# Hybrid GLA/Hyena encoder, float32: level factors in PSUM, one multiplication per level, blocks of 32 tokens, ScalarE scaling the head outputs

## The reference

```
h = rmsnorm(x);  q, k, v, r, g_lr, hyena = split(h @ w_in)
S_t = diag(exp(g_t)) S_{t-1} + k_t^T v_t ;  o_t = q_t S_t          # per head, g_t <= 0
o   = o_forward + o_backward                                        # over 256 tokens
o   = rmsnorm(o, per head) * silu(r)
x   = x + w_out([o ; hyena_group(...)])
x   = x + w_down(silu(h2 @ w_gate) * (h2 @ w_up)),  h2 = rmsnorm(x)
```

## Time and profile before

| | us |
|---|---|
| median of 3 runs | 1418.57 |
| the profiled execution, own time | 1420.57 |
| its span, first to last instruction | 1418.7 |
| PE busy | 1371.7 |
| DVE, ACT, POOL busy | 460.3, 479.1, 691.6 |
| layer 0, slots 4 to 24 | from 60 to 300 |
| layer 1, slots 4 to 24 | from 778 to 997 |

### The profile page before, as it was taken

One profiled execution on the slowest core, in us unless ns is written; L12 is line 12 of the kernel. 1 busy time (PEld: TensorE's weight loads), 2 busy tenths in 40 slices (PEclk: granted clock), 3 DMA queues, 4 the chain that ended last, 5 costly groups with the idle time before them and its releaser, 6 DMA issues.

```text
span 1418.7 us, 18349 instructions
## 1 busy us (share of the span) xinstructions
PE 1371.7 (97%) x7760; PEld 1096.4 (77%) x7760; DVE 460.3 (32%) x689; ACT 479.1 (34%) x740; POOL 691.6 (49%) x423
## 2 busy tenths in 40 slices
PE   6899999999999999999999899999999999999997
PEld 5566776788888778888876777777788888888885
DVE  5844855534022210000054776554250000000003
ACT  4644432233323223221246443322342223222122
POOL 2642753353555555544424665534625555554442
PEclk9999999999999999999999999999999999999999
DMA  6210111122323222332311211111222322233231
GB/s 234 87 44 32 60 33 59 44 67 82 127 90 104 89 90 81 113 104 90 103 60 47 73 46 61 61 45 33 86 75 89 104 96 97 90 117 105 90 104 75
DMA packets 31186, 116.63 MB, mean 82 GB/s; under 512 B 3456, under 2 KB 3584, under 8 KB 30720
## 3 DMA queue, kind: packets, MB, share of 16 engines
q1 hardware_dynamic: 31104, 115.45, 24.4%
HBM read 113.34 MB, written 2.10 MB: 81 GB/s over the span
## 4 chain that ended last, share of the span: by engine, by line
PE 85%; DVE 9%; ACT 2%; issue 1%; POOL 1%; DMA 1%; POOLq 0%; DVEq 0%; SPq 0%; ACTq 0%
PE ps L1098 16%; PE ps L1099 16%; PE ps L1100 16%; PE ps L1106 7%; PE ps L1109 7%; PE ps L1107 7%; PE ps L1314 4%; PE ps L1300 3%; PE ps L1128 2%; PE ps L1174 2%; DVE ring L925 1%; DVE ring L924 1%; PE ps L1235 1%; PE ps L1161 1%; PE ps L1261 1%
## 5 line engine op out<-in xcount | busy, mean ns | idle before, releaser
L692 POOL TENSOR_TENSOR w_lo<-w_raw,w_hi 128x1024 fp32r<-128x1024 f32 x192 | 464.1, 2418 | 412.8 <-ACT w_hi L417 412.8
L1098 PE MATMUL ps<-h_hi,w_hi 128*128 128x512 f32 (+1 forms) x1064 | 433.0, 407 | 0.4 <-POOL w_lo L692 0.4
L1100 PE MATMUL ps<-h_hi,w_lo 128*128 128x512 f32 (+1 forms) x1064 | 413.6, 389 | 0.0
L1099 PE MATMUL ps<-h_lo,w_hi 128*128 128x512 f32 (+1 forms) x1064 | 413.3, 388 | 0.0
L417 ACT ACTIVATE w_hi<-w_raw 128x1024 fp32r<-128x1024 f32 x192 | 201.7, 1051 | 197.8 <-PE ps L1109 193.6
L1098 PEld LDWEIGHTS ps<-h_hi,w_hi 128*128 128x128 f32 x1064 | 200.9, 189 | 48.8 <-issue 8.7
L1099 PEld LDWEIGHTS ps<-h_lo,w_hi 128*128 128x128 f32 x1064 | 200.7, 189 | 45.8 <-issue 7.2
L1100 PEld LDWEIGHTS ps<-h_hi,w_lo 128*128 128x128 f32 x1064 | 200.4, 188 | 42.1
L1072 DVE TENSOR_TENSOR hid<-ps,sg 128x512 f32<-128x512 f32 x44 | 30.4, 692 | 428.8 <-PE ps L1100 428.8
L1106 PE MATMUL ps<-w_hi,hid_hi 128*128 128x512 f32 x352 | 137.3, 390 | 1.9 <-POOL w_lo L692 1.9
L1107 PE MATMUL ps<-w_lo,hid_hi 128*128 128x512 f32 x352 | 137.0, 389 | 0.0
(11 more groups left out here) (154 smaller groups left out, 1559.4 us busy)
## 6 DMA issues: line engine op xcount, KB each, us to landing
w_raw<-in_units SPq DMA_DIRECT2D x198, 512.0 KB, 3.6
par<-in_par SPq DMA_DIRECT2D x2, 1310.5 KB, 9.7
gain<-in_gain SPq DMA_DIRECT2D x5, 512.0 KB, 4.8
x<-in_x SPq DMA_DIRECT2D x4, 512.0 KB, 7.2
out_y<-x SPq DMA_DIRECT2D x4, 512.0 KB, 2.6
cst<-in_cst SPq DMA_DIRECT2D x1, 1536.0 KB, 15.0
mask_f<-in_mask SPq DMA_DIRECT2D x1, 320.0 KB, 12.0
cst<-in_cst SPq DMA_DIRECT2D x1, 224.0 KB, 4.0
```

Source lines behind the costliest of these rows:

```text
L692: nc.gpsimd.tensor_tensor(w_tile(g, 1), w_raw[:, g % RAW], w_tile(g, 0).bitcast(F32), ALU.subtract).then_inc(s_lo, 1)
L1098: nc.tensor.matmul(out, hi, act_hi, start=start, stop=False)
L1099: nc.tensor.matmul(out, hi, act_lo, start=False, stop=False)
L1100: return nc.tensor.matmul(out, lo, act_hi, start=False, stop=stop)
```

## The change

1. The exponential of a level goes from `ring` to a PSUM bank instead of back to `ring`: banks 4 and 5 (`FB`), by the parity of the level number. ACT waits until DVE has used the factor two levels back.
2. DVE multiplies a whole level in one instruction: `pairs` is an access pattern that takes the lower halves from `g1` and the upper ones from `g2`; the result goes to `ring`.
3. All level results and the attention output share banks 2 and 3. Their columns are split: step 0, and the narrow results, in columns 0 to 255 or 0 to 383, level 1 and the attention output in 256 to 511.
4. The small blocks are of 32 tokens (`NEAR`) instead of 64. `near`, the masks and the put instructions are half as wide; PE runs the diagonal and the levels 3 to 7 in blocks of 32, twice as many matmuls of half the size.
5. The levels are dealt anew to the steps: (0), (1, 2), (3, 4, 5), (6, 7) instead of (0), (1, 2, 3), (4, 5), (6, 7). Level 3 loses its place in step 1, and step 2 has three levels. ACT does the third factor of a step behind the rounding of the slot's weight unit.
6. DVE runs `put_levels` ahead of `scaled`. PE runs `attend` ahead of the next head's step 0.
7. ACT scales the head outputs in 16 instructions in slot 22; DVE keeps the reciprocal (L1041).
8. `g12` starts at a multiple of 256 bytes from the base.

The core of the diff:

```diff
-STEPS = ((0,), (1, 2, 3), (4, 5), (6, 7))
+NEAR = 2 * MASKED[0]
+STEPS = ((0,), (1, 2), (3, 4, 5), (6, 7))
+PUTS = (0, 0, 0, 6)
-LA, LC = 2, 4
+LA, FB = 2, 4
+        place[0] += (base - place[0]) % 256
+        def pairs(h, s):
+            first = g1[:, h]
+            return bass.AP(first.tensor, first.offset,
+                           [list(first.ap[0]), [2 * s, TOK // (2 * s)], [HEADS * TOK + s, 2], [1, s]])
...
-            def factors(L, slot):
+            def factors(L, slot, late):
-                    for l in STEPS[hp[1]]:
+                    for l in STEPS[hp[1]][2:] if late else STEPS[hp[1]][:2]:
                         act.wait_ge(expo.sem, expo.at(L, n + 1))
-                        nc.scalar.activation(ring[:, n % FACT], ring[:, n % FACT], ACT.Exp,
+                        if n < 2:
+                            act.wait_ge(zmin.sem, zmin.at(L, HEADS))
+                        else:
+                            act.wait_ge(xld.sem, xld.at(L, n - 1))
+                        nc.scalar.activation(ps[:, FB + n % 2, :], ring[:, n % FACT], ACT.Exp,
                                              scale=1.0 / TEMP).then_inc(fact.sem, 1)
...
-                    factors(L, slot)
+                    factors(L, slot, False)
                     hi_unit(L * UNITS + slot + 2)
+                    factors(L, slot, True)
...
                     if slot == 22:
+                        act.wait_ge(o_inv.sem, o_inv.at(L, 1))
+                        for h in range(HEADS):
+                            for n in range(TT):
+                                k = TT * h + n
+                                last = nc.scalar.activation(v_tok[:, h, n], v_tok[:, h, n], ACT.Copy, scale=oss[:, k:k + 1])
+                            last.then_inc(osc.sem, 1)
                         hyena_square(L, 0)
...  # DVE, scaled
-                    f = split(ring[:, n % FACT], s)
-                    nc.vector.tensor_tensor(f[:, :, 0], split(g1[:, h], s)[:, :, 0], f[:, :, 0], ALU.mult)
-                    nc.vector.tensor_tensor(f[:, :, 1], split(g2[:, h], s)[:, :, 1], f[:, :, 1], ALU.mult)\
-                        .then_inc(xld.sem, 1)
+                    nc.vector.tensor_tensor(split(ring[:, n % FACT], s), pairs(h, s), split(ps[:, FB + n % 2, :], s),
+                                            ALU.mult).then_inc(xld.sem, 1)
...
+                    put_levels(L, slot)
                     scaled(L, slot)
-                    put_levels(L, slot)
...  # PE, level_step
-                        for e in range(2):
-                            cols = slice(P * n + BLOCK * e, P * n + BLOCK * e + BLOCK)
-                            nc.tensor.matmul(ps[BLOCK * e:BLOCK * e + BLOCK, LA, BLOCK * n:BLOCK * n + BLOCK],
-                                             g1[:, h, cols], g2[:, h, cols], start=True, stop=True)
+                        for e in range(0, P, NEAR):
+                            cols = slice(P * n + e, P * n + e + NEAR)
+                            nc.tensor.matmul(ps[e:e + NEAR, LA, NEAR * n:NEAR * n + NEAR], g1[:, h, cols], g2[:, h, cols],
+                                             start=True, stop=True)
...
-                        pe.wait_ge(put.sem, put.at(L, 10 * h + 2))
+                        pe.wait_ge(put.sem, put.at(L, 10 * h + PUTS[p]))
```

More of the change, by code:

```diff
@@ L547, in big_levels @@
                 act.wait_ge(pair.sem, pair.at(L, 4 * h + 2))
-                a = acs.next()
                 tiles = amat[:, 0].rearrange("p s j i -> p (s j) i")
-                forward, backward = (ps[:, LA + way, :].rearrange("p (l n c) -> p l n c", l=2, n=TT) for way in range(2))
-                nc.scalar.activation(near, forward[:, 0], ACT.Copy).then_inc(acs.sem, 1)
-                nc.scalar.activation(tiles[0:BLOCK, :, BLOCK:P], forward[0:BLOCK, 1], ACT.Copy)
-                nc.scalar.activation(tiles[BLOCK:P, :, 0:BLOCK], backward[BLOCK:P, 1], ACT.Copy)
-                act.wait_ge(acs.sem, a)
-                for rows in (slice(32, 64), slice(96, P)):
-                    last = nc.scalar.activation(near[rows, :, 0:32], backward[rows, 0, :, 0:32], ACT.Copy)
+                ways = [ps[:, LA + way, :] for way in range(2)]
+                nc.scalar.activation(near, ways[0][:, 0:TT * NEAR].rearrange("p (n c) -> p n c", n=TT), ACT.Copy)
+                for way in range(2):
+                    j, i = BLOCK * way, BLOCK * (1 - way)
+                    wide = ways[way][:, SEQ:2 * SEQ].rearrange("p (n c) -> p n c", n=TT)
+                    nc.scalar.activation(tiles[j:j + BLOCK, :, i:i + BLOCK], wide[j:j + BLOCK], ACT.Copy)
+                    for m in (0, BLOCK):
+                        j, i = m + NEAR * way, m + NEAR * (1 - way)
+                        narrow = ways[way][:, TT * NEAR:SEQ].rearrange("p (n c) -> p n c", n=TT)
+                        last = nc.scalar.activation(tiles[j:j + NEAR, :, i:i + NEAR], narrow[j:j + NEAR], ACT.Copy)
                 last.then_inc(big.sem, 1)
@@ L933, in put_levels @@
                 v.wait_ge(pair.sem, pair.at(L, 4 * h + p + 1))
-                if p == 1:
+                if p == 2:
                     v.wait_ge(big.sem, big.at(L, h + 1))
-                done = 10 * h + (0, 0, 2, 6)[p]
-                for l in (3,) if p == 1 else STEPS[p]:
+                done = 10 * h + PUTS[p]
+                for l in STEPS[p]:
                     for way in range(2):
@@ L1039, in _ @@
                         v.wait_ge(o_rms.sem, o_rms.at(L, 1))
[L1040 to L1047 removed]
+                        nc.vector.reciprocal(oss[:, :], oss[:, :]).then_inc(o_inv.sem, 1)
                     if slot == 24:
@@ L1198, in level_step @@
                             j, i = (low, up) if way == 0 else (up, low)
-                            last = nc.tensor.matmul(ps[:, LC + way, P * q:P * q + P], xl[rows, j], xl[rows, i],
+                            last = nc.tensor.matmul(ps[:, LA + way, P * q:P * q + P], xl[rows, j], xl[rows, i],
                                                     start=True, stop=True)
@@ L1226, in level_step @@
                     else:
-                        pe.wait_ge(put.sem, put.at(L, 10 * h + 2))
-                for l in (3,) if p == 1 else STEPS[p]:
-                    xl = ring[:, lvl(h, l) % FACT]
-                    for n in range(TT):
-                        for e in range(2):
-                            cols = slice(P * n + BLOCK * e, P * n + BLOCK * e + BLOCK)
-                            at = level_cols(l).start + BLOCK * n
-                            for way, rows in enumerate(ways):
-                                last = nc.tensor.matmul(
-                                    ps[BLOCK * e:BLOCK * e + BLOCK, level_bank(l) + way, at:at + BLOCK],
-                                    xl[rows, cols], xl[rows, cols], start=True, stop=True)
+                        pe.wait_ge(put.sem, put.at(L, 10 * h + PUTS[p]))
+                    for l in STEPS[p]:
+                        xl = ring[:, lvl(h, l) % FACT]
+                        for n in range(TT):
+                            for e in range(0, P, NEAR):
+                                cols = slice(P * n + e, P * n + e + NEAR)
+                                at = level_cols(l).start + NEAR * n
+                                for way, rows in enumerate(ways):
+                                    last = nc.tensor.matmul(ps[e:e + NEAR, LA + way, at:at + NEAR], xl[rows, cols],
+                                                            xl[rows, cols], start=True, stop=True)
                 last.then_inc(pair.sem, 1)
@@ L1329, in side @@
                 if at == 1:
+                    for h in range(HEADS):
+                        if slot == 4 * h + 8:
+                            attend(L, h)
                     hp = step_at(slot - 4)
@@ L1332, in side @@
                         level_step(L, *hp)
-                    for h in range(HEADS):
-                        if slot == 4 * h + 8:
-                            attend(L, h)
                     if slot == 22:
```

65 lines of the change are left out of this document (30 added, 35 removed).

## The result

The changed kernel takes 1408.07 us in the median of 4 runs (1407.15 to 1408.62), the kernel before 1420.00 beside it (4 runs, 1418.51 to 1422.59): a ratio of 0.9909, with a 95% interval of 0.9897 to 0.9920. It is faster by 12 to 13 us. The profiled execution has a span of 1405.4 us and 1407.15 of its own time, 13.4 less than the one before; the forecast for it was 1403.6.

A forecast was written before the change was run, and what follows sets the result against it. PE, busy 97% of the span, bounds the kernel, so only its waits and own work count. Waits 13.3, clock 4.5, PE's work -0.8: 17.0 us off 1420.57 gives 1403.6, median 1401.6; own range 1399 to 1408, 8-of-10 range 1396 to 1411.

The forecast's parts named there:

- DVE's multiplication: DVE's 128 multiplications become 64 of 512 columns with a source in PSUM, 0.65 us each; old pair 1.79 us.
- Puts: DVE's put instructions at half the columns: between 0.24 and 0.47 us each, 0.34 taken.
- L1286, 5.6: PE's wait for DVE's products in slot 19, both layers: 2.8 us each goes, gain 5.6 us.
- L1251, L1199, L1269, `oss`, 3.1: PE's smaller waits for DVE, 1.3, 0.8, 0.6 and 0.4 us: all gone, 3.1; at worst none.
- L1210, 3.2 with 0.3 left: PE's 3.5 us wait in slot 5, layer 1: scans end about 1.2 us sooner; gain 3.2, between 2.0 and 3.5.
- L1161, 1.4 of 4.6: PE's wait for `hidden_pair`, slot 5, layer 0: 1.4 of 4.6 us gained, between 0.6 and 2.4; low clock stays.
- The range: Forecast's own 1399 to 1408 us: waits give 10 to 14.5, clock 3.0 to 5.1, PE's work -3 to 0.
- the dear ends: Slot 19 with six puts at 2.8 us and two multiplications at 3.6: PE's wait of 2.8 us stays whole.
- Clock, 4.5: Three of four low-clock windows in PE's slots go, 1.5 us each: 4.5, at most 5.1, at least 3.0.
- PE's own work, -0.8: PE's smaller, more numerous matmuls in levels 3 to 7: +0.1 us a head, +0.8 for 8 heads, at most +9.
- B: Rival, PE's steps 2 and 3: each of 1408 added matmuls costs 17 ns, +24 us, 1425 us; chance 0.06.
- A, ACT binds: Rival: ACT's added 1.1 us a head makes PE wait before step 2 or `attend`: 1410 us; chance 0.12.

The follow-up runs named there:

- the two kernels above: The changed kernel with two half-width multiplications a level, factor still in PSUM: 1407.84 us; and with one multiplication, factor in SBUF: 1414.03 us.

## Why the prediction was right, and where it was off

The forecast was 1401.6, the time 1408.1: faster, as said, at the upper end of the forecast's own range of 1399 to 1408 and inside that of 1396 to 1411, but 6.5 us above. Of these, 3.5 are the profiled execution's (1407.15 for 1403.6); the rest is that the median lies 0.9 above that execution and not 2.0 below. That it was not further off is in part luck: 9.7 us of stops and low clock behind them were not foreseen, and some 6 us of gains (waits 2.1, borders 1.2, PE's work 1.3, the fourth low window 1.5) were not either. Step by step:

- *DVE's multiplication*, 0.65 taken and 0.65 to 0.70 named: 0.699. *Puts*, 0.34 taken: 0.30. The reason named, a source in PSUM, is shown by the two kernels above.
- *L1286, 5.6*: gone, with 0.6 us to spare where 0.3 was forecast. *L1251, L1199, L1269, `oss`, 3.1*: all gone. ACT's scaled copy takes 387 ns and not 0.27 us, which costs nothing.
- *L1210, 3.2 with 0.3 left*: the 3.5 went whole, by the way that was forecast. The two scans ahead of the multiplications take 1.79 us for 3.60, where 2.4 was expected: POOL's six short subtractions run until 776.16, and its unit work starts only there. PE's first matmul behind them is at 777.26, without a wait. Timeline of DVE, layer 1, against the earlier trace rows:

```profile
773.88 1.79 DVE L938 TENSOR_TENSOR_SCAN cum<-v_tok,u 128x256 f32<-128x256 f32 x2
775.70 1.28 DVE L952 TENSOR_TENSOR ring<-g,ps 128x512 f32<-128x512 f32 x2
```

- *L1161, 1.4 of 4.6, and its low clock to stay*: 2.1 went. L870 is L899 now and takes 0.66 us instead of 2.34, as DVE reaches it before POOL starts its 2.35 us unit work, at 65.79, which is the prediction's short item:

```profile
63.19 0.68 DVE L897 COPY hid_b<-hid_a 64x256 f32<-64x256 f32 x1
63.89 0.66 DVE L899 TENSOR_SCALAR hid_b<-hid_a 64x256 f32<-64x256 f32 x1
```

  The low clock behind it is absent here and in five other profiles, and present in five, with the same 2.9 us between two starts of PE in all of them; what decides it is open.
- A wait of 1.5 us in slot 4 of layer 0, for the first product, was left out of the sum; 0.4 of it stays, 1.1 gained. The row of before:

```profile
PE ps L1199 <- DVE ring L925: 1.5, 1, 1.5
```

- *The range*: its lower end for the waits, 10, is not the sum of the lower ends that the prediction names; 5.6 with 0, 2.0 and 0.6 is 8.2, and at the dear ends the 5.6 was to go as well. The text doesn't say how 10 comes about.
- *Clock, 4.5*: four windows went and not three, but two new ones came: about 3.
- *PE's own work, -0.8*: step 2 took 1.75 us ("about 1.7") and step 3 1.22 for 1.09, but step 1 1.39 for 2.24, each from start to the next start: about 0.06 us less a head, where 0.1 more was forecast. B, a price of 17 ns for each matmul, is refuted: a step 2 has 9 ns for each. With it falls, for this form, the floor of 25 ns that the prediction quoted from "TensorE: Matmul & The Clock Gate" of the Trainium skill.
- *A, ACT binds*: PE nowhere waited for `amat` or `near`; the smallest distance from the end of `big_levels` to step 2 was 1.04 us (783.28 to 784.32), for the 1.3 of the prediction.
- The step that failed is a term that wasn't there. *PE's own work* was priced by what a matmul takes when its instructions are at hand. The step's last sentence, that the steps are "long runs of one shape", was the danger and was read as the reassurance. 6.7 us of stops and 3 us of low clock come from it: without them the profiled execution would have been at 1397.4, by this count, 6 below the forecast.

The danger could have been seen ahead, though not its size. The page's third part has the queue of the instruction packets, and of before it says 62 packets, for 15,823 PE records with the semaphore instructions among them. In the trace of before, no two records 256 n + 152 and 256 n + 448 are less than 7.6 us apart, and a packet starts up to 10.9 us after the first of them. The change makes one burst of 384 instructions in 1.75 us.

What stays open: what starts a packet and makes it late (up to 5.6 us after record 256 n + 152 where a stop followed).

## What to carry to other kernels

Count the instructions of the longest burst of short ones, weight loads and semaphore instructions included, and set it against how fast they come: here 296 instructions had to last 2.3 to 7.8 us over the 34 stops, some 4 in most. A burst over that stops by its phase, so an unrelated edit anywhere ahead of it moves the time by several us; a wait named "issue" inside a block of one line is its mark. And when DVE is slow beside POOL, look for a source that can lie in PSUM before you look for fewer instructions.

## What the runs showed of the hardware

- PE's instructions arrive 256 at a time (73 packets of 16,384 bytes for 18,641 records), and all 34 stops were on a record of number 256 n + 192. PE went on 1.3 to 1.6 us after the packet's end in all of them.
- A short matmul that repeats the one ahead, same rows and same output, starts 32 ns after it; level 2's in turn take 11 ns each (48 records in 1.61 and 0.54 us), step 2's 9 and the diagonal's, on all 128 rows, 12. "TensorEngine Tiling (Array Packing)" in the Trainium skill, section "Key Properties", says that different tiles can load weights and multiply in parallel. The blocks agree; the 25 ns of the page "TensorE: Matmul & The Clock Gate" of the Trainium skill is near the 32 of the repeats, and not the 9.
- A block of the levels' shape put into a unit costs PE about 0.36 us beyond its matmuls: 0.09 ahead of it, 0.16 within it, 0.11 behind it.
- DVE's 128x512 product with both sources in SBUF takes 1.28 us in the mean of 64 (0.68 to 2.88, the long ones beside POOL's work) and 0.70 with one in PSUM (0.65 to 0.85).
